# Neighbourhood attention: who scales and masks the bias tables, GpSimd or VectorE

## The chip, the cores and the metric

One core of a Trainium2 chip runs the whole program. The metric is the device time of one execution in microseconds; the lower the better. TensorE (PE) multiplies matrices out of SBUF into PSUM, VectorE (DVE), ScalarE (ACT) and GpSimd (POOL) work elementwise, and SyncE (SP) issues the transfers. Each engine runs its own instructions in the order in which they were written; between engines, semaphores are counted up and waited for.

## The reference, cut to what matters

The program computes two transformer blocks on 512 tokens. The change touches one stage of the second layer of the first block, in which eight heads of dense attention (C) and eight heads of neighbourhood attention (D) run. The D heads add a relative-position bias to their scores and mask columns out of the window:

```
col_valid = (c[None, :] >= c0[:, None]) & (c[None, :] < c0[:, None] + D_WIN_C)
valid = jnp.tile(col_valid, (1, wr))
...
s = jnp.einsum('bqhd,bkhd->bhqk', q_row, k_win,
               preferred_element_type=jnp.float32) * scale
row_idx = r0 + jnp.arange(wr) - r + (D_WIN_R - 1)
bias = rpb_f[:, row_idx[None, :, None], col_idx[:, None, :]]
s = jnp.where(valid, s + bias.reshape(H, GRID_W, wr * GRID_W)[None], NEG)
p = jax.nn.softmax(s, axis=-1).astype(v.dtype)
return jnp.einsum('bhqk,bkhd->bqhd', p, v_win)
```

The kernel adds a table to the raw scores, (bias / scale) + mask, with the mask 0 or -1e30, and multiplies by scale afterwards.

## The kernel before, in words

`attention` (L1679) runs 32 units. A unit is two heads (a group) and one quarter (128) of the 512 queries. Groups 0 to 3 are the C heads (units 0 to 15), groups 4 to 7 the D heads (units 16 to 31). A unit passes through the engines as follows; every engine's order is fixed by a loop over i.

- TensorE: `score(i)` (L1745) into PSUM, then `turn(i-2)` (L1757), the transposition of the probabilities of unit i-2, which waits until they are scaled, then `values` (L1772), a quarter of the product with V of an older group. `score(u)` needs the maxima of unit u-2 (D heads) or its exponentials (C heads).
- VectorE: `peak(i)`, the row maxima. For a C unit that is two reductions (L1867) and a small multiplication (L1871); for a D unit two fused instructions (L1861) that read the scores in PSUM and the bias table in SBUF and write the sum to SBUF, each followed by a short read of the accumulator. Then `scale_rows(i-1)`: a reciprocal (L1876) and two multiplications in place in SBUF, one for each head (L1879, 128 rows by 512 columns each); I call the two the scaling pair of unit i-1. Once in four units it also copies a finished group out (L1899).
- ScalarE: the copy of transposed probabilities (L1811), then the exponentials of unit i (L1826).

The bias tables are 8 heads of 128 x 896 float32 (448 KB each). They lie in four slots of the buffer `bias`. SyncE issues heads 0 to 3 at the stage's start, and heads 4 and 5, and 6 and 7, once the maxima of the group that used the slots before are done (L1905 to L1912). Heads 0 and 1 belong to group 4 (units 16 to 19), heads 2 and 3 to group 5, 4 and 5 to group 6 (from unit 24), 6 and 7 to group 7 (from unit 28).

Before the change, VectorE turns each table into (bias / scale) + mask itself, in `shape_bias` (L1837 to L1843), one instruction for each head. It stands behind `peak(i)` and ahead of `scale_rows(i-1)`, at i = 14 and 15 for heads 0 and 1, 18 and 19 for heads 2 and 3, 22 and 23, 26 and 27. GpSimd does nothing in this stage. In the whole program it has 22 small instructions: constants at the start, 16 copies of 128 x 2 in the first attention stage (L1729), and two memsets much later (L3685, L3686).

Of the kernel before, what the change touches and what calls it, by code (L numbers as in the profile page):

```python
# [17 lines left out]
ALU = mybir.AluOpType  # L18
# [4 lines left out]
P = 128  # L23
# [10 lines left out]
GRID = 64  # L34
WIN_C = 16
REL = 14
# [1256 lines left out]
class Net:  # L1293
# [385 lines left out]
    def attention(self, groups, kb, opened, evac, fill=None, weights=None, late=None):  # L1679
# [7 lines left out]
        s, ps = self.s, self.ps  # L1687
        g, sets = len(groups[0].q), 4 // len(groups[0].q)
        units = [(p, qt) for p in range(len(groups)) for qt in range(4)]
        n = len(units)  # L1690
        shaped = [groups[p].shaped for p, _ in units]
        nk = groups[0].k[0][0].shape[-1] // P
        bias_heads = [h for gr in groups for h in gr.bias or ()]
        with ExitStack() as ctx:
            tag, p = self.names, self.place
# [4 lines left out]
            bs = p(f'bias{tag}', [P, 4, REL * GRID], kb + 6.5 * g * nk) if bias_heads else None  # L1700
# [12 lines left out]
            def width(u):  # L1713
                k0, k1 = span(u)
                return (k1 - k0) * P

            @block.gpsimd
            def _(pool):
                done = 0
                for u, (p, qt) in enumerate(units):  # L1720
                    gr = groups[p]
                    if gr.sink is None:
                        continue
                    if not done:
                        pool.wait_ge(*s['copied'].at(sum(gr.sink is not None for gr in groups)))
                    if shaped[u - 2]:
                        pool.wait_ge(*s['exped'].at(u - 1))
                    w, at = width(u), 2 * sum(gr.sink is not None for gr in groups[:p])
                    pool.tensor_copy(sb[:, u % 2, :, w], ns[:, at:at + 2]).then_inc(*s['pool'].up())  # L1729
                    done += 1  # L1730
# [100 lines left out]
            @block.vector  # L1831
            def _(dve):
                sinks = [gr.sink for gr in groups if gr.sink is not None]
                for i, sink in enumerate(sinks):
                    dve.tensor_scalar(ns[:, 2 * i:2 * i + 2], sink, -1.0, None, ALU.mult).then_inc(*s['copied'].up())

                def shape_bias(p, j):  # L1837
                    h = groups[p].bias[j]
                    dve.wait_ge(*s[f'biasin{h % 4}'].at(16 * (h // 4 + 1)))
                    v = bs[:, h % 4, :].rearrange("p (a b) -> p a b", b=GRID)  # L1840
                    m = self.c('colmask')[:, None, :].to_broadcast([P, REL, GRID])
                    dve.scalar_tensor_tensor(out=v, in0=v, scalar=1.0 / groups[p].scale, in1=m, op0=ALU.mult,
                                             op1=ALU.add).then_inc(*s['vec'].up())  # L1843

                def peak(u):
                    p, qt = units[u]
                    gr, w = groups[p], width(u)
                    dve.wait_ge(*s['scored'].at(u + 1 - opened))
                    if shaped[u]:
                        if u >= 2 and shaped[u - 2]:  # L1850
                            dve.wait_ge(*s['exped'].at(u - 1))
                    for j in range(g):
                        src = ps[:, bank(u, j), 0:w]
                        if shaped[u]:
                            a = (6 - 2 * qt) * GRID
                            add = bs[:, gr.bias[j] % 4, a:a + w] if gr.bias else gr.mask(qt)
                            first = -NEG
                            if gr.sink is not None:
                                at = 2 * sum(gr.sink is not None for gr in groups[:p])
                                first = ns[:, at + j:at + j + 1]  # L1860
                            dve.tensor_tensor_reduce(sb[:, u % 2, j, 0:w], src, add, -gr.scale, first, ALU.add, ALU.min,  # L1861
                                                     stat_of(u, 1, j)).then_inc(*s['maxed' if j == g - 1 else 'vec'].up())
                        elif gr.folded:
                            dve.tensor_reduce(stat_of(u, 1, j), src, AX.X, ALU.max,
                                              negate=True).then_inc(*s['maxed' if j == g - 1 else 'vec'].up())
                        else:
                            dve.reduce_max(stat_of(u, 0, j), src, AX.X).then_inc(*s['vec'].up())  # L1867
                    if shaped[u] or gr.folded:
                        return
                    dve.wait_ge(*s['vec'].now())  # L1870
                    dve.tensor_scalar(stat(u, 1), stat(u, 0), -gr.scale, None, ALU.mult).then_inc(*s['maxed'].up())  # L1871

                def scale_rows(u):
                    gr, w = groups[units[u][0]], width(u)
                    dve.wait_ge(*s['exped'].at(u + 1))
                    dve.reciprocal(stat(u, 3), stat(u, 2)).then_inc(*s['vec'].up())  # L1876
                    dve.wait_ge(*s['vec'].now())
                    for j in range(g):
                        ins = dve.tensor_scalar(pr[:, u % 3, j, 0:w], pr[:, u % 3, j, 0:w], stat_of(u, 3, j), None, ALU.mult)  # L1879
                    ins.then_inc(*s['scaled'].up())  # L1880

                for i in range(n + 6):
                    if i < n:
                        peak(i)
                    if i + 2 < n and units[i + 2][1] in (0, 1) and groups[units[i + 2][0]].bias:
                        shape_bias(units[i + 2][0], units[i + 2][1])
                    if evac and i == 2:
                        evac.dve(dve, evac.late)
                    if late and i in (2, 3):
                        late[1](dve, i - 2)  # L1890
                    if 0 <= i - 1 < n:
                        scale_rows(i - 1)
                    p, part = divmod(i - 6, 4)
                    if weights and i == n:
                        weights(dve)
                    if p >= 0 and part == 3:
                        dve.wait_ge(*s['weighted'].at(p + 1))
                        for at, dst in groups[p].dst:
                            ins = dve.tensor_copy(dst, ps[:, at, :])  # L1899
                        ins.then_inc(*s['headout'].up())  # L1900
                self.last_head = len(groups[-1].dst), s['headout'].at(len(groups))
                self.mem_free = self.last_head[1]
# [2122 lines left out]
```

## Time and profile before

| | |
|---|---|
| time, median of 3 runs | 2836.95 us (2836.83 to 2837.25) |
| the profiled execution's own time | 2837.87 us |
| its span | 2836.6 us |
| granted TensorE clock, mean | 0.999 |
| TensorE busy | 2789.8 us (98% of the span) |
| VectorE busy | 1673.1 us (59%) |
| GpSimd busy | 5.0 us, 22 instructions |
| the attention stage of the change, from its first unit in `attention` to its last product | 879.3 to 991.8 us |

The profiled execution took 2837.87 us: its span of 2836.6 us and 1.27 us around it. It lies 0.92 us above the median of the runs. A row of a timeline gives start and duration in us, engine, line, operation, the buffers written and read, shapes, and in brackets how long the engine stood idle before it and what ended that. Where one row covers two instructions (x2), the duration is from the start of the first to the end of the second; on VectorE the second can start a little before the first is through.

### The profile page before, as it was taken

To read this page: it belongs to the slowest core of one execution; us is meant where nothing else is said; L and a number is where in the kernel's file an instruction comes from. 1 tells how busy PE (TensorE), PEld (TensorE's weight loads), DVE (VectorE), ACT (ScalarE), POOL (GpSimd) and SP (SyncE) were. 2 spreads that over 40 slices of the span, in tenths; PEclk is the share of its full clock that TensorE was granted. 3 is DMA by queue.
4 is the path that set the end of the run, shared out by engine and by line. 5 is a ranking of instruction groups with operands and counts; after the bars stand their busy time and mean duration, and the time that the engine had idled before them with its cause. 6 is when DMAs were issued, how large, how long until landed. Compare 5 with 4: busy or idle time off the path is not lost.

```text
span 2836.6 us, 38710 instructions
## 1 busy us (share of the span) xinstructions
PE 2789.8 (98%) x15838; PEld 2059.1 (73%) x15838; DVE 1673.1 (59%) x3425; ACT 651.4 (23%) x1349; POOL 5.0 (0%) x22
## 2 busy tenths in 40 slices
PE   9999999999999999999999999999999999999998
PEld 3557588888644486788887557777776877788887
DVE  5686554453344874655754876766656536766654
ACT  5651310100134613211100022522221102222200
POOL 0000000000000000000000000000000000000000
PEclk9999999999999999999999999999999999999999
DMA  4013122222221132222222122211113321222222
GB/s 150 30 39 118 52 82 90 89 97 90 91 73 55 34 119 75 75 89 89 90 89 97 61 68 75 97 52 48 48 46 134 118 91 53 81 90 89 85 93 82
DMA packets 63535, 228.59 MB, mean 81 GB/s; under 512 B 7168, under 2 KB 9472, under 8 KB 62592
## 3 DMA queue, kind: packets, MB, share of 16 engines
q1 hardware_dynamic: 63360, 226.14, 23.5%
q8 instruction: 125, 2.05, 0.3%
q14 instruction: 50, 0.41, 0.0%
HBM read 221.91 MB, written 4.19 MB: 80 GB/s over the span
## 4 chain that ended last, share of the span: by engine, by line
PE 93%; DVE 5%; issue 1%; ACT 0%; DMA 0%; SPq 0%; DVEq 0%; ACTq 0%
PE ps L1990 30%; PE ps L711 19%; PE ps L1385 9%; PE ps L2026 8%; PE ps L1397 5%; PE ps L1772 3%; PE ps L1745 2%; PE ps L1428 2%; PE ps L1466 2%; PE ps L1757 2%; PE ps L743 1%; PE ps L2574 1%; PE ps L2595 1%; PE ps L2805 1%; PE ps L3494 1%
## 5 line engine op out<-in xcount | busy, mean ns | idle before, releaser
L1990 PE MATMUL ps<-h,ring 128*128 128x256 f32 x1136 | 269.0, 380 | 3.9 <-ACT q_p L2124 2.0
L1990 PEld LDWEIGHTS ps<-h,ring 128*128 128x128 f32 x1136 | 214.9, 190 | 37.9 <-issue 8.7
L1990 PE MATMUL ps<-h_sums,w_sums 128*128 128x256 f32 x1008 | 224.4, 379 | 0.0
L1990 PEld LDWEIGHTS ps<-h_sums,w_sums 128*128 128x128 f32 x1008 | 191.5, 190 | 26.0
L711 PE MATMUL ps<-hid_sums,d_sums 128*128 128x256 f32 x740 | 175.8, 379 | 0.5 <-DVE hid_sums L1949 0.5
L711 PEld LDWEIGHTS ps<-hid_sums,d_sums 128*128 128x128 f32 x740 | 140.5, 190 | 19.9 <-issue 0.8
L1931 DVE TENSOR_TENSOR d_sums<-ring 128x512 f32<-128x512 f32 (+1 forms) x51 | 33.6, 659 | 167.8 <-DMA ring<-stream_dram 167.6
L1990 PE MATMUL ps<-c_h_sums,c_sums 128*128 128x256 f32 x504 | 112.2, 379 | 0.0
L967 ACT ACTIVATE d_xsq<-x 128x512 f32<-128x512 f32 x47 | 28.1, 621 | 363.2 <-DVE x L928 354.9
L1757 PEld LDWEIGHTS ps<-constants,probs 128*128 128x128 f32 x560 | 62.4, 141 | 62.2 <-DVE probs L1879 47.5
L1990 PEld LDWEIGHTS ps<-c_h_sums,c_sums 128*128 128x128 f32 x504 | 95.8, 190 | 13.0
L1385 PE MATMUL ps<-h,ring 128*128 128x512 f32 x240 | 104.9, 593 | 0.0
L1811 ACT ACTIVATE probsT<-ps 128x512 f32<-128x512 f32 (+2 forms) x176 | 82.8, 508 | 90.9 <-PE ps L1757 90.5
L1757 PE MATMUL ps<-constants,probs 128*128 128x128 f32 x560 | 82.7, 279 | 10.3 <-DVE probs L1879 9.6
L711 PE MATMUL ps<-hid_sums,ring 128*128 128x256 f32 x370 | 87.9, 379 | 0.0
L1385 PEld LDWEIGHTS ps<-h,ring 128*128 128x128 f32 x240 | 45.5, 190 | 56.9 <-issue 56.1
L711 PE MATMUL ps<-hid,ring 128*128 128x256 f32 x352 | 82.5, 379 | 0.0
L711 PE MATMUL ps<-hid,d_sums 128*128 128x256 f32 x352 | 82.5, 379 | 0.0
L3911 DVE SCALAR_TENSOR_TENSOR c_conv<-c_x,vectors,c_conv 128x511 f32<-128x511 f32 (+1 forms) x88 | 62.1, 747 | 34.1 <-ACT c_conv L3859 33.3
L1990 PE MATMUL ps<-h_sums,ring 128*128 128x256 f32 x336 | 79.4, 379 | 0.0
L1990 PE MATMUL ps<-h,w_sums 128*128 128x256 f32 x336 | 79.4, 379 | 0.0
L711 PEld LDWEIGHTS ps<-hid_sums,ring 128*128 128x128 f32 x370 | 70.3, 190 | 9.6
(724 smaller groups left out, 5215.1 us busy)
## 6 DMA issues: line engine op xcount, KB each, us to landing
ring<-stream_dram SPq DMA_DIRECT2D x395, 512.0 KB, 3.8
bias<-bias_dram SPq DMA_DIRECT2D x8, 448.0 KB, 4.5
mem<-mem_dram SPq DMA_DIRECT2D x3, 1024.0 KB, 5.7
x_kept_dram<-x SPq DMA_DIRECT2D x1, 2048.0 KB, 10.1
x<-x_kept_dram SPq DMA_DIRECT2D x1, 2048.0 KB, 7.8
out_dram<-x SPq DMA_DIRECT2D x16, 128.0 KB, 1.9
x<-x_dram SPq DMA_DIRECT2D x3, 512.0 KB, 7.8
rope_ab<-ropes_dram SPq DMA_DIRECT2D x4, 256.0 KB, 8.0
```

Source lines behind the costliest of these rows:

```text
L711: mm = pe.matmul(self.region(q, at), w(j), x(k), start=opens, stop=last and j == len(ks) - 1, skip_group_check=True)
L1385: mm = pe.matmul(out, w, r, start=(k == 0), stop=(k == len(rhs) - 1))
L1397: mm = pe.matmul(out, w, r, start=(k == 0), stop=(k == len(rhs) - 1))
L1428: mm = pe.matmul(out, l, w, start=(k == 0), stop=(k == len(lhs) - 1))
L1466: mm = pe.matmul(self.ps[:, m % 4, :], self.next_block(pe), src[k], start=(k == 0), stop=(k == len(src) - 1))
L1745: mm = pe.matmul(ps[:, bank(u, j), 0:(k1 - k0) * P], gr.q[j][i][:, qt * P:(qt + 1) * P], gr.k[j][i][:, k0 * P:k1 * P], start=(i == 0), sto ...
L1757: mm = pe.transpose(ps[:, turn_bank(u, j), b * P:(b + 1) * P], pr[:, u % 3, j, b * P:(b + 1) * P], self.c('ident'))
L1772: mm = pe.matmul(ps[at:at + rows, to, c], gr.v(b, j)[i], pt[:, p % 2, j, b, c], start=(b == 0), stop=(b == nk - 1), skip_group_check=True)
L1811: ins = act.activation(pt[:, p % 2, j, k0:k1, qt * P:(qt + 1) * P], ps[:, turn_bank(u, j), 0:(k1 - k0) * P].rearrange("p (b q) -> p b q", ...
L1990: mm = pe.matmul(ps[:, bank + at, 0:256], w(k), x(k), start=start and k == 0, stop=k == 3, skip_group_check=not start)
L2026: mm = pe.matmul(ps[:, bank, part], w(k), x(k), start=n in (0, 2) and k == 0, stop=k == 3, skip_group_check=True)
L3911: ins = dve.scalar_tensor_tensor(out=out, in0=xs[:, f % 2, j, 0:S - lag], scalar=self.v('conv', (2 - lag) * 2 * FT + FT * j + f), in1=out, ...
```

## The change

VectorE's `shape_bias` goes, and with it its eight instructions. GpSimd now walks through all eight heads in order, at the head of its part of the stage: it waits for the head's transfer, multiplies the table in place by 1/scale, waits for that, and adds the mask in place. VectorE waits for the second of a group's two heads at the group's first `peak`.

```
             @block.gpsimd
             def _(pool):
+                for gr in groups:
+                    for h in gr.bias or ():
+                        pool.wait_ge(*s[f'biasin{h % 4}'].at(16 * (h // 4 + 1)))
+                        v = bs[:, h % 4, :].rearrange("p (a b) -> p a b", b=GRID)
+                        pool.tensor_scalar(v, v, 1.0 / gr.scale, None, ALU.mult).then_inc(*s['pool'].up())
+                        pool.wait_ge(*s['pool'].now())
+                        pool.tensor_tensor(v, v, self.c('colmask')[:, None, :].to_broadcast([P, REL, GRID]),
+                                           ALU.add).then_inc(*s['biased'].up())
...
-                def shape_bias(p, j):
-                    h = groups[p].bias[j]
-                    dve.wait_ge(*s[f'biasin{h % 4}'].at(16 * (h // 4 + 1)))
-                    v = bs[:, h % 4, :].rearrange("p (a b) -> p a b", b=GRID)
-                    m = self.c('colmask')[:, None, :].to_broadcast([P, REL, GRID])
-                    dve.scalar_tensor_tensor(out=v, in0=v, scalar=1.0 / groups[p].scale, in1=m, op0=ALU.mult,
-                                             op1=ALU.add).then_inc(*s['vec'].up())
-
                 def peak(u):
                     p, qt = units[u]
                     gr, w = groups[p], width(u)
                     dve.wait_ge(*s['scored'].at(u + 1 - opened))
+                    if gr.bias and qt == 0:
+                        dve.wait_ge(*s['biased'].at(bias_heads.index(gr.bias[1]) + 1))
...
                 for i in range(n + 6):
                     if i < n:
                         peak(i)
-                    if i + 2 < n and units[i + 2][1] in (0, 1) and groups[units[i + 2][0]].bias:
-                        shape_bias(units[i + 2][0], units[i + 2][1])
```

On VectorE, where the C units end and the D units begin (i = 14 to 16), this stood before; `stats` holds the maxima and sums, `probs` the probabilities, `shaped` the sums of scores and bias, and an ISA row with `ps,bias` is one of the fused instructions of `peak`:

```order
L1871 TENSOR_SCALAR stats_5551<-stats_5551 128x2 [waits vec]
L1842 SCALAR_TENSOR_TENSOR bias_5550<-bias_5550,constants 128x896 [waits biasin0]
L1876 RECIPROCAL stats_5551<-stats_5551 128x2 [waits exped]
L1879 TENSOR_SCALAR probs_5547<-probs_5547,stats_5551 128x512 [waits vec]
L1879 TENSOR_SCALAR probs_5547<-probs_5547,stats_5551 128x512
L1867 TENSOR_REDUCE stats_5551<-ps 128x1 [waits scored]
L1867 TENSOR_REDUCE stats_5551<-ps 128x1
L1871 TENSOR_SCALAR stats_5551<-stats_5551 128x2 [waits vec]
L1842 SCALAR_TENSOR_TENSOR bias_5550<-bias_5550,constants 128x896 [waits biasin1]
L1876 RECIPROCAL stats_5551<-stats_5551 128x2 [waits exped]
```

The same place now (the lines have moved down by two):

```order
L1873 TENSOR_SCALAR stats_5551<-stats_5551 128x2 [waits vec]
L1878 RECIPROCAL stats_5551<-stats_5551 128x2 [waits exped]
L1881 TENSOR_SCALAR probs_5547<-probs_5547,stats_5551 128x512 [waits vec]
L1881 TENSOR_SCALAR probs_5547<-probs_5547,stats_5551 128x512
L1869 TENSOR_REDUCE stats_5551<-ps 128x1 [waits scored]
L1869 TENSOR_REDUCE stats_5551<-ps 128x1
L1873 TENSOR_SCALAR stats_5551<-stats_5551 128x2 [waits vec]
L1878 RECIPROCAL stats_5551<-stats_5551 128x2 [waits exped]
L1881 TENSOR_SCALAR probs_5547<-probs_5547,stats_5551 128x512 [waits vec]
L1881 TENSOR_SCALAR probs_5547<-probs_5547,stats_5551 128x512
L1863 ISA shaped_5549,stats_5551<-ps,bias_5550 128x512 [waits biased,scored]
```

The reciprocal and the scaling pair now follow directly on the maxima, and the first fused instruction of the group has taken on the wait for `biased`.

On GpSimd nothing stood between the copies of the first attention stage and the memsets. Now there stands (heads 0 and 1 shown; heads 2 to 7 follow in the same form, ahead of the memsets):

```order
L1737 COPY shaped_607<-sinks_609 128x2 [waits exped] x14
L1723 ISA
L1723 TENSOR_SCALAR bias_5550<-bias_5550 128x896 [waits biasin0]
L1725 TENSOR_TENSOR bias_5550<-bias_5550,constants 128x896 [waits pool]
L1723 TENSOR_SCALAR bias_5550<-bias_5550 128x896 [waits biasin1]
L1725 TENSOR_TENSOR bias_5550<-bias_5550,constants 128x896 [waits pool]
```

Eight instructions of VectorE have become sixteen of GpSimd, and one without a buffer (the ISA row) stands ahead of them with nothing to wait for. The orders of TensorE, ScalarE and SyncE are as before.

## Rows read from the trace of the kernel before

**Rows 1.** The page: busy time of an engine, and the chain that ended last.
```profile
PE 2789.8 (98%) x15838; PEld 2059.1 (73%) x15838; DVE 1673.1 (59%) x3425; ACT 651.4 (23%) x1349; POOL 5.0 (0%) x22
...
PE 93%; DVE 5%; issue 1%; ACT 0%; DMA 0%; SPq 0%; DVEq 0%; ACTq 0%
```

**Rows 2.** Timeline of TensorE, the scores of units 16 to 21.
```profile
928.69 1.13 PE L1745 MATMUL ps<-k_d,q_d 64*128 64x512 f32 x4
...
932.48 1.13 PE L1745 MATMUL ps<-k_d,q_d 64*128 64x512 f32 x4
...
935.57 1.13 PE L1745 MATMUL ps<-k_d,q_d 64*128 64x512 f32 x4
...
938.66 1.13 PE L1745 MATMUL ps<-k_d,q_d 64*128 64x512 f32 x4
...
942.14 1.13 PE L1745 MATMUL ps<-k_d,q_d 64*128 64x512 f32 x4
...
945.36 1.13 PE L1745 MATMUL ps<-k_d,q_d 64*128 64x512 f32 x4
```

**Rows 3.** Timeline of VectorE at i = 15: a table, then the scaling pair.
```profile
928.32 1.08 DVE L1842 SCALAR_TENSOR_TENSOR bias<-bias,constants 128x896 f32<-128x896 f32 x1
...
929.51 0.88 DVE L1879 TENSOR_SCALAR probs<-probs,stats 128x512 f32<-128x512 f32 x2
```

**Rows 4.** Groups of instructions, 870 to 990 us: busy us, mean ns.
```profile
L1879 DVE TENSOR_SCALAR probs<-probs,stats 128x512 f32<-128x512 f32 x62 | 27.3, 483 | 1.1
...
L1842 DVE SCALAR_TENSOR_TENSOR bias<-bias,constants 128x896 f32<-128x896 f32 x8 | 8.7, 1087 | 0.0
...
L1899 DVE COPY q_c<-ps 128x512 f32<-128x512 f32 x4 | 2.7, 682 | 0.0
```

**Rows 5.** Timeline of GpSimd: its longest instruction.
```profile
1691.53 1.81 POOL L3686 MEMSET gla_att<- 128x2048 f32 x1
```

**Rows 6.** Timeline of VectorE beside that instruction.
```profile
1691.96 0.27 DVE L3607 MEMSET gla_state<- 128x256 f32 x1
1692.14 0.63 DVE L2049 TENSOR_TENSOR rw_sums<-ring 128x512 f32<-128x512 f32 x1
```

**Rows 7.** Busy time by stretch (PE, PEld, DVE, ACT, POOL), clock, DMA share, GB/s.
```profile
884.00:886.00 2.00, 1.67 (x10) 1.32 (x11) 1.93 (x6) 1.04 (x4) 0.00 (x0) 1.00 0.29 117
...
945.00:947.00 2.00, 2.00 (x11) 0.89 (x10) 1.09 (x3) 1.94 (x6) 0.00 (x0) 1.00 0.11 40
```

**Rows 8.** The tile `bias`: transfers from issue to landing, all eight.
```profile
DMA to landing us min/median/max: 3.4/4.5/6.7
```

**Rows 9.** Timeline of VectorE: the scaling pairs of units 1 to 4.
```profile
883.39 0.88 DVE L1879 TENSOR_SCALAR probs<-probs,stats 128x512 f32<-128x512 f32 x2
...
885.77 0.88 DVE L1879 TENSOR_SCALAR probs<-probs,stats 128x512 f32<-128x512 f32 x2
...
888.77 0.88 DVE L1879 TENSOR_SCALAR probs<-probs,stats 128x512 f32<-128x512 f32 x2
...
891.55 0.88 DVE L1879 TENSOR_SCALAR probs<-probs,stats 128x512 f32<-128x512 f32 x2
```

**Rows 10.** Timeline of TensorE: the turns of units 1 to 4, and of unit 20.
```profile
884.33 1.09 PE L1757 MATMUL ps<-constants,probs 128*128 128x128 f32 x8 [0.57 <-DVE probs L1879]
...
886.98 1.04 PE L1757 MATMUL ps<-constants,probs 128*128 128x128 f32 x8
...
889.75 1.04 PE L1757 MATMUL ps<-constants,probs 128*128 128x128 f32 x8
...
892.49 1.09 PE L1757 MATMUL ps<-constants,probs 128*128 128x128 f32 x8
...
949.51 1.09 PE L1757 MATMUL ps<-constants,probs 128*128 128x128 f32 x8
```

**Rows 11.** Timeline of VectorE: the scaling pair of unit 20, and unit 24's first fused instruction.
```profile
947.96 0.88 DVE L1879 TENSOR_SCALAR probs<-probs,stats 128x512 f32<-128x512 f32 x2
...
956.20 0.69 DVE L1861 CUSTOM_DVE_ANT_0 shaped<-ps,bias 128x512 f32<-128x512 f32 x1
```

## The prediction

> **What bounds the kernel now.** I read the page first. TensorE is busy for 98% of the span, the chain that ended last runs through it for 93% and through VectorE for 5%, and transfers have no share [rows 1]. So a microsecond is won or lost only where TensorE waits, and what is won in one stage stays won, as no transfer stands behind it in the chain.
>
> Then the timeline of TensorE in the changed stage, taken by the starts of its scores. In the D heads a unit takes 3.09 us where nothing disturbs it (935.57 to 938.66). It takes more at the places of `shape_bias`: units 16 to 17 take 3.79, units 19 to 20 3.48 and 20 to 21 3.22 [rows 2]. These are excesses of 0.70, 0.39 and 0.13 us. The last two come again in the same size at heads 4 and 5 and at 6 and 7, a pattern that I read three times. The timeline of VectorE shows why: 1.08 us of table stand directly ahead of the scaling pair at 929.51, whose end at 930.39 TensorE's turn waits for [rows 3].
>
> Last I read the stage's start (879 to 893 us), where TensorE has no products with V yet and its units are short. There turns 1 to 4 begin 0.06, 0.33, 0.10 and 0.06 us behind the end of the scaling pair that they need (pairs start at 883.39, 885.77, 888.77, 891.55 and last 0.88; turns start at 884.33, 886.98, 889.75, 892.49) [rows 9, 10]. Nothing can be slipped into VectorE there. This matters since the first four tables land just then.
>
> **What is removed.** Eight instructions of 1.09 us, 8.7 us of VectorE [rows 4]. On TensorE's path lie 0.70 + 3 x (0.39 + 0.13) = 2.26 us [rows 2]. Without the table at i = 15, the pair starts some 1.0 us sooner, at 928.5, ends at 929.4, and turn 14 can follow its score 16 (928.69 and 1.06 of it) at 929.75. What is late next is nothing: TensorE's own 3.09 us a unit bound it, as between units 18 and 19. The remaining 6.4 us of the 8.7 stood in VectorE's idle time and are worth nothing.
>
> **What is added on GpSimd.** Sixteen instructions of 128 x 896. No row shows one that reads a tensor of this size. The nearest row of the engine is a memset of 128 x 2048 in 1.81 us, 0.88 ns a column [rows 5]: 0.79 us for one pass over 896 columns. The nearest row of the shape is VectorE's own 1.09 us [rows 4]. Lower bound for each kind: 0.79. Upper bound, if each operand and the result were a pass by itself: two passes, 1.6 us, for the multiplication, and three, 2.4 us, for the addition. I take 0.9 for the multiplication (between the two nearest rows) and twice that, 1.8, for the addition, which reads two operands; with 0.1 for the wait between them, 2.8 us a head, against bounds of 1.7 and 4.1.
>
> The Trainium skill ("GPSIMD Engine Reference", section "Elementwise — side-by-side cycle accounting") gives an addition of two tensors some 2.6 cycles a column at 1.2 GHz; an estimate by it is 1.94 us for 896 columns. With it every meeting with an addition, below, would be up to 0.14 us dearer. No run here shows it.
>
> The instruction without a buffer ahead of them on GpSimd has 700 us of idle time before the first table, and costs nothing, whatever it does. The memsets behind them wait for 1691 us anyway [rows 5].
>
> **When they run.** The four first tables are 1.8 MB, and the transfers are through at 884.6 us (29% of the stretch from 884) [rows 7]. The first can land 3.4 us after its issue at 877.3 [rows 8]; I take 881 us. From there GpSimd is busy to some 895, exactly beside the stage's start. Heads 4 and 5 land by 945.2 (11% of the stretch from 945) [rows 7] and are wanted at 956.20 [rows 11]: 11 us for 5.6 us of work, hidden. Heads 6 and 7 have the same room, 13 us later. Units 16 and 24 wait for `biased`, which has come long before; behind this wait would stand the pair of the unit before, and TensorE behind that.
>
> **The disputed cost: both engines in SBUF at once.** The scaling pair goes from SBUF to SBUF: two instructions of 0.48 us in 0.88 us, so one in 0.40 [rows 3, 4]. A copy of the same 512 columns out of PSUM takes 0.68 alone [rows 4]. So the pair moves data at nearly twice the rate, by a second way into SBUF that the other forms do not use. Whether that way is free while GpSimd reads, no row shows. The nearest rows are VectorE's fast memset (0.18 us from start to start for 256 columns) and an addition of 0.63 us, both undisturbed beside GpSimd's memset [rows 6]; but that one only writes. Bounds: nothing, or every pair waits until the running GpSimd instruction is through, and between its halves for another one. I take the middle: a pair that meets a running instruction waits for its end, then passes whole. The reason is the pair's rate, which the undisturbed addition does not have; the memset's evidence lowers the chance, not the size.
>
> The Trainium skill ("SBUF — State Buffer", section "Who interferes with whom") says that VectorE in a two-port mode and GpSimd take turns on a shared pair of ports, each for a whole instruction, and that copies and multiplications by a scalar from SBUF to SBUF enter such a mode. By it the sum is the one below; without it, 2834.7. The undisturbed rows 6 do not contradict it where it speaks of two SBUF inputs (these collide only with reads of GpSimd), and no row tests the rest.
>
> Walked through at the start, with 0.9 and 1.8:
> - GpSimd: multiplication 881.0 to 881.9, addition to 883.8. Pair 1, due 883.39, waits 0.41; turn 1 is 0.35 late.
> - GpSimd, after that pair: 884.7 to 885.6, 885.7 to 887.5. Pair 2, due 885.77 + 0.41 = 886.2, waits 1.3, is 1.7 late; turn 2 had 0.33 of room: 1.4 late.
> - GpSimd: 888.4 to 889.3, 889.4 to 891.2. Pair 3, due 888.77 + 1.4 = 890.2, waits 1.0; turn 3 is 2.3 late.
> - GpSimd: 892.1 to 893.0, 893.1 to 894.9. Pair 4, due 891.55 + 2.3 = 893.9, waits 1.0; turn 4 is 3.3 late. The first four tables are done.
>
> So +3.3 us, never given back, as TensorE bounds what follows. In the D heads the pair of unit 20 ends at 948.84 and its turn starts at 949.51, a room of 0.67 [rows 10, 11]. Two pairs in each of two stretches meet GpSimd. A pair falling at random into an addition of 1.8 us costs beyond its room 1.13 x 1.13 / 2 / 1.8 = 0.35 us on average, and additions are two thirds of GpSimd's time: 0.25 a pair, 1.0 for four (0 to 4.5).
>
> **The sum.** -2.3 + 3.3 + 1.0 = +2.0 us. On the profiled execution that is 2837.87 + 2.0 = 2839.9 us; the median of the runs stands 0.92 lower, so 2839.0 us.
>
> **Rivals.**
> - No contest in SBUF. Then the gain stands alone: 2836.95 - 2.3 = 2834.7 us. For it: rows 6. Against it: the pair's doubled rate. If GpSimd alone gave way, the result is the same, since it has 11 us for 5.6.
> - GpSimd gets in between the halves of a pair. This ends on the other side. A GpSimd instruction that has waited during the first half starts before the second. From pair 1 on each pair then passes two instructions of GpSimd: the rest of one (about 1.0) and a whole one (0.9 or 1.8, mean 1.35), 3 x 2.35 = 7.0 for pairs 2 to 4, and 0.4 + 0.9 for pair 1, less 0.5 of room: 7.8 us. In the D heads two stretches cost 1.5 each. Sum: -2.3 + 7.8 + 3.0 = +8.5, so 2845.4 us. It counts as slower once the waits pass 8.0 us. For it: GpSimd's request is the older one. Against it: the second half starts 0.08 us before the first is through, so VectorE may never let go.
> - Tables late. Four instructions must fit between 945.2 and 956.20; more than 5.4 us a head, above my upper bound of 4.1 unless GpSimd itself is held up, would stop unit 24. At 6.0 it costs 1.2 in each of two stretches: 2836.95 - 2.3 + 2.4 = 2837.1 without any other wait, and about 2846 with the waits of the rival before.
>
> **How the numbers follow.** Forecast 0.43, with a range of its own from 2837 to 2842.5. No contest 0.33. Between the halves 0.20. Late tables 0.03. Something else 0.01. The range 2834.4 to 2846.0 holds the first three but for the upper half of the third, where GpSimd's durations lie near their upper bounds (1.6 and 2.4 instead of 0.9 and 1.8 would make each wait a third longer or more). About what a measurement of this kernel can tell from no change is 0.2%, 5.7 us. Faster by more than that needs a gain over 5.7 us, and only 2.26 are there: 0.02. Slower by more: most of the third case, and the upper end of the fourth and first: 0.21. Within: 0.77.
>
> **What would show it.** In the profile after: (1) the D units at 3.09 us from score to score at the places where 3.79, 3.48 and 3.22 stood; wrong if VectorE is late there for another reason. (2) GpSimd at 0.8 to 1.6 and 0.8 to 2.4 us an instruction. (3) For the forecast: the pairs of units 1 to 4 start late, or their instructions last over 0.48 us, each ending behind a GpSimd instruction, and TensorE idles some 3 us more between 884 and 896. If all 62 keep 0.48 us while GpSimd runs, the first rival holds. If the two halves of a pair lie more than 0.5 us apart with a GpSimd instruction between them, the second. (4) Units 24 and 28 show no wait for GpSimd; one would be the last rival. The prediction as a whole is wrong if a stage outside 879 to 992 us changes its length.

## The result and the profile after

The changed kernel takes 2850.02 us (median of 6 runs, 2848.23 to 2851.29) against 2837.06 us (6 runs, 2836.74 to 2837.25) for the one before: a ratio of 1.0046, 95% interval 1.0035 to 1.0056. It is 13.0 us slower where +2.0 was forecast with a range up to 2846.0. The profiled execution took 2850.39 us, its span 2848.9 us, 12.3 more than before. The first line of its page and the groups of the stage, over 870 to 1000 us (busy us, mean ns), answer to [rows 1, 4]:

```profile
PE 2791.8 (98%) x15838; PEld 2059.9 (72%) x15838; DVE 1684.2 (59%) x3417; ACT 651.3 (23%) x1349; POOL 41.9 (1%) x38
```
```profile
L1881 DVE TENSOR_SCALAR probs<-probs,stats 128x512 f32<-128x512 f32 x62 | 45.6, 777 | 1.1
...
L1723 POOL TENSOR_SCALAR bias<-bias 128x896 f32<-128x896 f32 x8 | 20.1, 2511 | 763.4 <-DMA bias<-bias_dram 763.0
...
L1725 POOL TENSOR_TENSOR bias<-bias,constants 128x896 f32<-128x896 f32 x8 | 16.8, 2102 | 0.7
```

VectorE lost eight instructions and is busy for 11 us more; the mean of the multiplications of the scaling pairs has gone from 483 to 777 ns. On GpSimd the multiplication takes 2.5 us and the addition 2.1.

The timelines of GpSimd and of VectorE at the stage's start:

```profile
880.69 2.45 POOL L1723 TENSOR_SCALAR bias<-bias 128x896 f32<-128x896 f32 x1 [704.05 <-DMA bias<-bias_dram]
883.22 2.12 POOL L1725 TENSOR_TENSOR bias<-bias,constants 128x896 f32<-128x896 f32 x1
885.42 2.51 POOL L1723 TENSOR_SCALAR bias<-bias 128x896 f32<-128x896 f32 x1
888.01 2.12 POOL L1725 TENSOR_TENSOR bias<-bias,constants 128x896 f32<-128x896 f32 x1
```
```profile
882.34 1.08 DVE L1881 TENSOR_SCALAR probs<-probs,stats 128x512 f32<-128x512 f32 x1
...
883.34 2.28 DVE L1881 TENSOR_SCALAR probs<-probs,stats 128x512 f32<-128x512 f32 x1
...
887.12 3.29 DVE L1881 TENSOR_SCALAR probs<-probs,stats 128x512 f32<-128x512 f32 x2
```

The two halves of the first pair are shown singly. The first is taken up at 882.34 and is through at 883.42, 0.28 us behind the end of GpSimd's multiplication (883.14). The second is taken up at 883.34, but GpSimd's addition has stood ready since 883.22. The addition goes first, ends at 885.34, and the half is through at 885.62, again 0.28 us behind it. The next pair has the same picture 4.8 us later. A pair lasts 3.3 us instead of 0.88 [rows 9], and a unit takes 4.8 us, the time of one head on GpSimd. TensorE, turns of units 1 to 4, then a product with V:

```profile
885.68 1.09 PE L1765 MATMUL ps<-constants,probs 128*128 128x128 f32 x8 [3.10 <-DVE probs L1881]
...
890.47 1.09 PE L1765 MATMUL ps<-constants,probs 128*128 128x128 f32 x8 [0.43 <-DVE probs L1881]
...
895.27 1.09 PE L1765 MATMUL ps<-constants,probs 128*128 128x128 f32 x8 [1.99 <-DVE probs L1881]
...
900.07 1.66 PE L1765 MATMUL ps<-constants,probs 128*128 128x128 f32 x8 [1.99 <-DVE probs L1881]
901.66 1.98 PE L1780 MATMUL ps<-probsT,v_c 128*64 128x512 f32 x4
```

The last two rows are slow by themselves (1.66 where 1.09 is usual, 1.98 where 1.08). The stretches show why; their last columns are the granted clock, the share of the transfers and GB/s:

```profile
888.00:890.00 2.00, 2.00 (x3) 0.34 (x1) 2.00 (x2) 1.23 (x4) 1.99 (x1) 0.50 0.00 0
...
902.00:904.00 2.00, 2.00 (x5) 0.42 (x2) 0.40 (x2) 2.00 (x6) 0.00 (x0) 0.54 0.01 4
```

A granted clock of 0.50 is TensorE at 1.2 GHz instead of 2.4. It fell behind the idle time of 3.10 us and once more behind the two of 1.99. The first fall lies in a wait for VectorE and costs nothing (the idle time at 890.47 is only 0.43 for that reason); the second lengthens the stage.

In the D heads, the scores of units 16, 17 and 20 to 24, which answer to [rows 2], and among them the two turns that waited:

```profile
937.86 1.13 PE L1753 MATMUL ps<-k_d,q_d 64*128 64x512 f32 x4
...
940.95 1.13 PE L1753 MATMUL ps<-k_d,q_d 64*128 64x512 f32 x4
...
950.22 1.13 PE L1753 MATMUL ps<-k_d,q_d 64*128 64x512 f32 x4
...
953.32 1.13 PE L1753 MATMUL ps<-k_d,q_d 64*128 64x512 f32 x4
...
956.46 1.13 PE L1753 MATMUL ps<-k_d,q_d 64*128 64x512 f32 x4
...
959.20 1.09 PE L1765 MATMUL ps<-constants,probs 128*128 128x128 f32 x8 [1.60 <-DVE probs L1881]
...
961.23 1.13 PE L1753 MATMUL ps<-k_d,q_d 64*128 64x512 f32 x4
...
963.28 1.09 PE L1765 MATMUL ps<-constants,probs 128*128 128x128 f32 x8 [0.93 <-DVE probs L1881]
...
965.32 1.13 PE L1753 MATMUL ps<-k_d,q_d 64*128 64x512 f32 x4
```

The gain is there: 3.09 us from unit 16 to 17 where 3.79 stood, and 3.10 from 20 to 21 where 3.22 stood. But units 22 to 23 take 4.77 and 23 to 24 take 4.09, beside heads 4 and 5 on GpSimd; the same comes again beside heads 6 and 7.

Here a pair also meets the beginning of a multiplication on GpSimd (VectorE, GpSimd):

```profile
952.83 1.55 DVE L1881 TENSOR_SCALAR probs<-probs,stats 128x512 f32<-128x512 f32 x2
```
```profile
953.05 2.57 POOL L1723 TENSOR_SCALAR bias<-bias 128x896 f32<-128x896 f32 x1 [53.32 <-DMA bias<-bias_dram]
```

The pair is through at 954.38, while the multiplication runs until 955.62. So a half does not always wait for GpSimd's instruction to end. The section on the hardware comes back to this.

For the comparisons I cut the stage in two in the timeline of TensorE. The start runs from the score of unit 2 (879.28 before, 878.11 after) to that of unit 16 (928.69, 937.86). The rest runs on to the last row of products with V, sixteen at once (988.17, 1000.55). Behind the stage nothing changed: from that row to the span's end it is 1848.4 us in both. Start and rest are read from one profiled execution of each kernel, so they and the medians need not add up to the last microsecond. For e7_only_add the profiled execution, 2841.40 us, is the fastest of ten; for e5_one_after it is 1.0 us above the median.

| kernel | time, us | against the kernel before, us | start, us | rest, us |
|---|---|---|---|---|
| before | 2837.06 | | 49.41 | 59.48 |
| changed | 2850.02 | +13.0 | 59.75 | 62.69 |
| e1_no_shaping | 2835.27 | -1.5 | 49.41 | 57.23 |
| e2_both | 2855.43 | +18.7 | 58.87 | 67.99 |
| e4_accum_before | 2843.97 | +7.2 | 51.16 | 64.17 |
| e4_accum_after | 2842.29 | +5.5 | 55.68 | 58.58 |
| e8_all_slow | 2836.98 | +0.2 | 50.65 | 58.59 |
| e5_one_before | 2840.38 | +3.5 | 50.41 | 62.07 |
| e5_one_after | 2842.78 | +5.9 | 57.02 | 59.27 |
| e6_later | 2844.42 | +7.5 | 53.94 | 62.70 |
| e3_memsets | 2843.32 | +6.6 | 54.00 | 61.52 |
| e7_only_add | 2843.17 | +6.4 | 54.15 | 59.69 |
| v2_early | 2834.50 | -2.4 | 49.41 | 57.23 |
| v2_again | 2834.58 | -2.2 | 49.41 | 57.24 |

Times are medians; the kernel before ran anew beside each group of experiments (2836.75, 2836.89 and 2836.76 us).

### The profile page after: what moved, and what is told of

It is laid out like the page before. It is cut to its first block, busy times and chain, and to the rows that moved or that the text cites. A ratio compares the mean times of both kernels' runs of the same rounds, so it can differ in the third digit from the quotient of the medians.

```text
span 2848.9 us, 38721 instructions
## 1 busy us (share of the span) xinstructions
PE 2791.8 (98%) x15838; PEld 2059.9 (72%) x15838; DVE 1684.2 (59%) x3417; ACT 651.3 (23%) x1349; POOL 41.9 (1%) x38
## 4 chain that ended last, share of the span: by engine, by line
PE 93%; DVE 5%; issue 1%; ACT 0%; DMA 0%; SPq 0%; DVEq 0%; ACTq 0%
PE ps L1990 30%; PE ps L711 19%; PE ps L1385 9%; PE ps L2026 8%; PE ps L1397 5%; PE ps L1780 3%; PE ps L1753 2%; PE ps L1428 2%; PE ps L1466 2%; PE ps L1765 2%; PE ps L743 1%; DVE probs L1881 1%; PE ps L2574 1%; PE ps L2595 1%; PE ps L2805 1%
## 5 line engine op out<-in xcount | busy, mean ns | idle before, releaser
L1881 DVE TENSOR_SCALAR probs<-probs,stats 128x512 f32<-128x512 f32 (+2 forms) x176 | 88.5, 533 | 4.0
```

## The experiments

The theory after the result: VectorE's fast form of multiplication (0.40 us for 512 columns from SBUF to SBUF) and GpSimd take turns in SBUF, and all of the loss comes from these waits. The main rivals: the wait for `biased` (late tables), the moved order on VectorE, and a fixed price of TensorE's lower clock.

**e1_no_shaping: no engine makes the tables.** Against the kernel before:

```
+                    if gr.bias and qt == 0:
+                        for h in gr.bias:
+                            dve.wait_ge(*s[f'biasin{h % 4}'].at(16 * (h // 4 + 1)))
...
-                    if i + 2 < n and units[i + 2][1] in (0, 1) and groups[units[i + 2][0]].bias:
-                        shape_bias(units[i + 2][0], units[i + 2][1])
```

> No engine scales and masks the tables: the eight instructions of VectorE are gone and nothing is put on GpSimd; VectorE only waits for the transfers (the scaling by 1/scale and the column mask are left out of the computation). Theory (turns in SBUF: VectorE's removal is worth 2.26 us, and the loss comes from GpSimd's instructions): 2.3 us faster than before, 2834.8 us, D units at 3.09 us throughout. Rival (what VectorE's order or the added waits do is the loss): slower than before, by up to 13 us.

Measured 2835.27 us, ratio 0.9995 (0.9985 to 1.0004). The interval cannot tell it from before, and the median lies 1.5 us under where 2.3 were expected. The trace is clearer: the rest of the stage is 2.25 us shorter (57.23 against 59.48), the start the same. So in the stage the removal is worth what the forecast said, and the order on VectorE is not the loss.

**e2_both: the tables stay on VectorE, and GpSimd does the same work for nobody.**

```
+                for gr in groups:
+                    for h in gr.bias or ():
+                        pool.wait_ge(*s[f'biasin{h % 4}'].at(16 * (h // 4 + 1)))
...
+                        pool.tensor_scalar(spare[:, :], self.cst[:, 0:REL * GRID], 8.0, None, ALU.mult).then_inc(*s['pool'].up())
+                        pool.wait_ge(*s['pool'].now())
+                        v = spare[:, :].rearrange("p (a b) -> p a b", b=GRID)
+                        pool.tensor_tensor(v, v, self.c('colmask')[:, None, :].to_broadcast([P, REL, GRID]),
+                                           ALU.add).then_inc(*s['biased'].up())
```

> The kernel before, with VectorE's shaping in place, and beside it GpSimd does sixteen instructions of the same two forms and size at the same times, from the constants into a spare buffer that nobody reads or waits for. Theory (turns in SBUF): GpSimd alone costs what the changed kernel lost plus the gain: 13 + 2.3 = some 15 us slower than before (2852 us), with scaling pairs of 3.3 us at units 1 to 4. Rival (tables late, or the wait for 'biased'): nobody waits for GpSimd here, so the time is that of before, 2837 us.

Measured 2855.43 us, +18.7 (ratio 1.0065, 1.0050 to 1.0080), against some 15 expected. Nobody waits for GpSimd here by a semaphore, and all of the loss is there. The surplus over 15 lies in the rest of the stage. VectorE's own table instructions, with two inputs in SBUF each, wait as well: two of the eight met an addition of GpSimd and took 2.62 and 2.63 us. Groups of that kernel; the means were 483 and 1087 ns before [rows 4]:

```profile
L1890 DVE TENSOR_SCALAR probs<-probs,stats 128x512 f32<-128x512 f32 x62 | 42.9, 734 | 1.1
...
L1853 DVE SCALAR_TENSOR_TENSOR bias<-bias,constants 128x896 f32<-128x896 f32 x8 | 11.8, 1470 | 0.0
```

**e4_accum_before and e4_accum_after: the pair in a slower form.** The same edit on the kernel before and on the changed one:

```
-                        ins = dve.tensor_scalar(pr[:, u % 3, j, 0:w], pr[:, u % 3, j, 0:w], stat_of(u, 3, j), None, ALU.mult)
+                        acc = dict(scalar2=0.0, op1=ALU.add, accum_out=stat_of(u, 4, j)) if bias_heads else dict(scalar2=None)
+                        ins = dve.tensor_scalar(pr[:, u % 3, j, 0:w], pr[:, u % 3, j, 0:w], stat_of(u, 3, j), op0=ALU.mult, **acc)
```

> The kernel before with the same other form of the scaling pair: the control. Both theories: each pair 0.4 to 0.5 us longer, which only costs where TensorE waits for it (the first four units, and the units beside a table): 2 to 5 us over before, 2839 to 2842 us.

> The changed kernel with the scaling pair of this stage in another form: each multiplication also adds a zero and sums its row into an unused statistic. Theory (only the fast form, 0.40 us for 512 columns, has to take turns with GpSimd): the pair runs at 0.6 us each, does not wait for GpSimd, and the time is within 1 us of e4_accum_before minus 2.3 us. Rival (every instruction of VectorE that reads and writes SBUF waits for GpSimd): 10 us or more above e4_accum_before.

The control costs 7.2 us (expected 2 to 5): a half takes 0.74 us, and VectorE is short of time beside each table. With the pairs in this form the changed kernel is 1.7 us faster than its control, 2842.29 against 2843.97. All 62 halves keep 744 ns in both, GpSimd or not. What still waited at the start was an instruction I had not thought of, the multiplication of the maxima, 128 x 2 (timelines of VectorE and GpSimd in e4_accum_after):

```profile
888.01 1.93 DVE L1873 TENSOR_SCALAR stats<-stats 128x2 f32<-128x2 f32 x1
```
```profile
887.84 2.07 POOL L1725 TENSOR_TENSOR bias<-bias,constants 128x896 f32<-128x896 f32 x1
```

It takes 0.17 us alone and is through 0.03 us behind GpSimd's addition. TensorE keeps its full clock in this run (1.00 in every stretch of 2 us from 880 to 920), and the start still costs 4.5 us more than its control's, 55.68 against 51.16: the waits cost time without any fall of the clock.

**e8_all_slow: that one in the slower form too** (the pairs as in e4_accum_after).

```
-                    dve.tensor_scalar(stat(u, 1), stat(u, 0), -gr.scale, None, ALU.mult).then_inc(*s['maxed'].up())
+                    acc = dict(scalar2=0.0, op1=ALU.add, accum_out=stat_of(u, 4, 0)) if bias_heads else dict(scalar2=None)
+                    dve.tensor_scalar(stat(u, 1), stat(u, 0), -gr.scale, op0=ALU.mult, **acc).then_inc(*s['maxed'].up())
```

> e4_accum_after, with the small multiplication of the C units' maxima (128 x 2) in the slower form too. In e4_accum_after that multiplication was the only instruction of VectorE that still waited (up to 1.9 us) and the start still cost some 3.5 us more than in its control. Theory (only the fast form takes turns, whatever its size): no instruction of VectorE waits for GpSimd any more, and the time falls from 2842.3 to 2838 to 2839 us, 5 us under e4_accum_before, which pays for its tables on VectorE. Rival (something else at the start waits for GpSimd): it stays at 2842 us.

Measured 2836.98 us, 7.0 under its control, e4_accum_before (5 were expected), and level with the kernel before (ratio 1.0001, 0.9991 to 1.0010). GpSimd does all its sixteen instructions in this run. The start falls from 55.68 to 50.65 us. Groups:

```profile
L1883 DVE TENSOR_SCALAR_CACHE_REDUCE probs<-probs,stats 128x512 f32<-128x512 f32 x62 | 43.8, 744 | 1.1
...
L1723 POOL TENSOR_SCALAR bias<-bias 128x896 f32<-128x896 f32 x8 | 19.6, 2451 | 752.9 <-DMA bias<-bias_dram 752.5
...
L1874 DVE TENSOR_SCALAR_CACHE_REDUCE stats<-stats 128x2 f32<-128x2 f32 x14 | 2.2, 155 | 0.5
```

This settles the cause: with the same work on GpSimd at the same time, no wait for it is left once VectorE's fast form is gone. The halves keep the 744 ns of the control, and the start is no longer than there (50.65 against 51.16). A kernel in this form with no tables at all was not run.

**e5_one_before and e5_one_after: the pair as one instruction.**

```
+                    if bias_heads:
+                        ins = dve.tensor_tensor(pr[:, u % 3, :, 0:w], pr[:, u % 3, :, 0:w],
+                                                stat(u, 3)[:, :, None].to_broadcast([P, g, w]), ALU.mult)
-                    for j in range(g):
+                    for j in () if bias_heads else range(g):
```

> The kernel before with the scaling pair as that one instruction: the control. Both theories: 0.25 us longer a unit on VectorE, 0 to 2 us over before.

> The changed kernel with the scaling pair of this stage as one instruction that multiplies both heads by their reciprocals (two inputs in SBUF, 1024 columns, about 1.1 us). Theory (a turn is taken for each instruction, and GpSimd gets in between the halves): one instruction waits once, for the rest of one GpSimd instruction (up to 2.5 us) and no more; the loss against e5_one_before is about half of the changed kernel's, 3 to 7 us. Rival (two inputs in SBUF need no turn): 2 us faster than e5_one_before. Rival (the wait is for all of GpSimd's work in hand): as slow as the changed kernel, 2850 us.

The control costs 3.5 us (expected 0 to 2); the changed kernel in this form is 2.4 above its control (expected 3 to 7). Its start loses 6.6 us (57.02 against 50.41) where the pairs in halves lost 10.3. How much of that is one wait instead of two, this run cannot say, since the edit changes the form as well. The pair at 885.42 is through at 887.39, 0.44 us ahead of the end of GpSimd's multiplication (885.38 to 887.83), so it did not wait for that end; and up to 1.4 us at a time went to the multiplication of the maxima, which is still in the fast form. 1.65 us of the 6.6 are the lower clock (0.50 in 898 to 900). In the D heads GpSimd's multiplication was stretched, so far that unit 24 waited for its tables, the last rival of the forecast (e5_one_after, VectorE, then GpSimd):

```profile
885.42 1.97 DVE L1881 TENSOR_TENSOR probs<-probs,stats 128x1024 f32<-128x1024 f32 x1
...
962.26 0.69 DVE L1863 CUSTOM_DVE_ANT_0 shaped<-ps,bias 128x512 f32<-128x512 f32 x1 [2.07 <-POOL bias L1725]
```
```profile
950.02 3.20 POOL L1723 TENSOR_SCALAR bias<-bias 128x896 f32<-128x896 f32 x1 [50.64 <-DMA bias<-bias_dram]
```

**e6_later: heads 0 to 3 in the quiet part of the C units.**

```
+                        if h == 0:
+                            pool.wait_ge(*s['exped'].at(2))
+                            for _ in range(2):
...
+                            pool.wait_ge(*s['exped'].at(9))
```

(The lines left out are a multiplication and an addition on a spare buffer.)

> The changed kernel, but GpSimd starts with heads 0 to 3 only after the exponentials of unit 8, when the C units run at 3.80 us and a scaling pair ends 1.13 us before its turn. Ahead of that, while VectorE is idle (869 to 880 us), GpSimd runs two multiplications and two additions of the same size on a spare buffer. Theory (turns): pairs are still stretched to 3.3 us, 2.4 more, of which 1.1 is room: 1.3 us for each of four or five units, so the start costs 5 to 7 us instead of 10.3, and the whole is 2844 to 2847 us. Rival (the start is dear because TensorE falls to its lower clock there): the same 10 us are lost wherever the tables are made. The four instructions alone show what GpSimd takes without VectorE: theory of turns, some 2.4 and 1.8 us, since the 2.1 of the additions then holds a wait for half a pair; rival, 2.5 and 2.1 as beside VectorE.

Measured 2844.42 us, within the expected 2844 to 2847; the start loses 4.5 us (expected 5 to 7) instead of 10.3, and the rest is as in the changed kernel, 62.70 against 62.69. So the price depends on the place. But the time came out in part by luck, as the waits were not those expected: only the first pair was stretched to 3.4 us, the next two lasted 1.56 (at 911.91 and 916.60), and the multiplication of the maxima waited instead (1.80 us at 919.39). The clock fell here too (0.50 in 910 to 912); the product and the score that it stretched, by 0.45 and 1.20 us, are 1.65 of the 4.5. GpSimd's instructions alone:

```profile
867.45 2.45 POOL L1725 TENSOR_SCALAR spare<-constants 128x896 f32<-128x896 f32 x1 [691.00 <-ACT probs L1845]
869.98 2.07 POOL L1728 TENSOR_TENSOR spare<-spare,constants 128x896 f32<-128x896 f32 x1
```

They take 2.45 and 2.07 us with VectorE idle (it has nothing between 866.9 and 879.8). My 1.8 for the addition was wrong: 2.07 is its own time, and GpSimd is hardly held up by the pairs.

**e3_memsets: GpSimd only writes.** The kernel before, with four fills for each head:

```
+                        pool.wait_ge(*s[f'biasin{h % 4}'].at(16 * (h // 4 + 1)))
+                        pool.memset(spare[:, :], 0.0).then_inc(*s['pool'].up())
+                        pool.wait_ge(*s['pool'].now())
...
```

> The kernel before, and beside it GpSimd fills a spare buffer, four fills of 128 x 896 for each head in place of the multiplication and the addition: it writes and reads nothing (0.8 us each, 3.2 us a head against 4.7). Theory (the fast form needs both ways in and out of SBUF, so any work of GpSimd takes turns with it): the scaling pairs of units 1 to 4 wait up to 0.8 us for each half, 0.5 to 1 us each unit, and the time is 2 to 6 us over before. Rival (only reads of GpSimd are in the way, as the fast fill of VectorE ran undisturbed beside GpSimd's memset): pairs keep 0.88 us and the time is that of before.

Measured 2843.32 us, +6.6 (ratio 1.0023, 1.0014 to 1.0032), a little over the expected 2 to 6; a pair of its start (VectorE) beside a fill of GpSimd:

```profile
889.61 2.16 DVE L1891 TENSOR_SCALAR probs<-probs,stats 128x512 f32<-128x512 f32 x2
```
```profile
889.59 0.84 POOL L1725 MEMSET spare<- 128x896 f32 x1
```

The fast form waits for writes as well. The table instruction of VectorE does not: its eight keep a mean of 1086 ns, and one that began with a fill (955.07, the fill from 955.08 to 955.92) took 1.08 us, where in e2_both two that met an addition took 2.6. The clock stayed at 1.00 in the whole stage, and the start lost 4.6 us all the same. That VectorE's own fast fill ran undisturbed beside GpSimd's memset [rows 6] said nothing about the pairs.

**e7_only_add: the addition alone.** The multiplication on GpSimd and the wait behind it are left out:

```
-                        pool.tensor_scalar(v, v, 1.0 / gr.scale, None, ALU.mult).then_inc(*s['pool'].up())
-                        pool.wait_ge(*s['pool'].now())
```

> The changed kernel with the addition of the mask alone on GpSimd; the multiplication by 1/scale is left out of the computation. GpSimd's work falls from 4.7 to 2.2 us a head. Theory (turns): the loss goes with the number and length of GpSimd's instructions: about 4 us at the start instead of 10.3, 1 instead of 2.7 in each of the two later stretches, less the gain of 2.3: 3 to 5 us over before, 2840 to 2842 us. Rival (a fixed price for having GpSimd in the stage): near 2850 us.

Measured 2843.17 us, +6.4 where 3 to 5 were expected. The start loses 4.7 us and the rest 2.5 against e1_no_shaping: about half of the changed kernel's 10.3 and 5.5, as GpSimd's time has halved. So the loss follows the time that GpSimd works and is not a fixed price for having it in the stage. One part does not follow it: TensorE's clock fell once (0.50 in 886 to 888) and stretched a turn and a score by 0.78 and 0.95 us, together 1.7, near the 1.6 of the changed kernel.

**v2_early: the tables on VectorE at better places.** The kernel before, with `shape_bias` behind the scaling pair instead of ahead of it, heads 0 to 3 at i = 10 to 13, heads 4 to 7 at 22, 23, 26 and 27 (left out: the wait for the tables at a group's first `peak`, and the old call of `shape_bias`):

```
+                early = [(p, j, 10 + 2 * (p - first) + j if p < first + 2 else 4 * p - 2 + j)
+                         for p in range(first, len(groups)) for j in range(g)]
...
                     if 0 <= i - 1 < n:
                         scale_rows(i - 1)
+                    for p, j, at in early:
+                        if i == at:
+                            shape_bias(p, j)
```

> VectorE makes the tables, as before, but at other places: behind the scaling pair instead of ahead of it, heads 0 to 3 at i = 10 to 13, where VectorE has 1.32 us of idle time in each C unit, and heads 4 and 5 at i = 22 and 23, 6 and 7 at i = 26 and 27. Theory (the 2.26 us were lost only because a table stood ahead of a pair that was wanted): 1.5 to 2.3 us faster than before, 2834.7 to 2835.5 us. Rival (VectorE is short of time in the stage): as before.

> v2_early once more, in more rounds, for the size of its gain: VectorE makes the tables behind the scaling pair, heads 0 to 3 early. Theory: 2.3 us under before, as in the first run (2834.5 against 2836.9). Rival (the first run's difference was noise): within 1 us of before.

Measured 2834.50 us, ratio 0.9992 (0.9983 to 1.0002), and again 2834.58 us, 0.9992 (0.9983 to 1.0001): 2.4 and 2.2 us under the kernel before. Each interval just reaches no change, but the two runs agree with each other and with the trace. There the stage is as short as with no tables at all, 49.41 and 57.23 us (scores of units 16 and 17):

```profile
927.18 1.13 PE L1745 MATMUL ps<-k_d,q_d 64*128 64x512 f32 x4
930.27 1.13 PE L1745 MATMUL ps<-k_d,q_d 64*128 64x512 f32 x4
```

It is the fastest kernel here that computes the whole reference, and it leaves GpSimd idle.

## Why the prediction was wrong

**What bounds the kernel, and the gain: right.** 2.26 us were forecast; e1_no_shaping and v2_early show 2.25 in the rest of the stage, and 1.5 and 2.4 in the medians. In the changed kernel, units 16 to 17 run at 3.09 us.

**The disputed cost: the right mechanism, and the wrong step in it.** Contest in SBUF was forecast, and it decides: e2_both has it without any dependence, e8_all_slow has the dependence without the contest. The step that failed is "a pair that meets a running instruction waits for its end, then passes whole". Each half waits by itself, and GpSimd gets in between, as the rival on the other side had it (chance 0.20, 2845.4 us). My reason against that rival, that the second half is taken up before the first is through, holds in the rows (883.34 against 883.42) and did not help: GpSimd's addition had been ready 0.12 us longer (883.22) and went first. In the D heads the step fails the other way too: there halves got through before GpSimd's multiplication had ended (954.38 against 955.62). The Trainium skill ("SBUF — State Buffer", section "Who interferes with whom") has the exclusive turn for a whole instruction and the multiplication by a scalar among the forms that take it, and that the form which also writes its accumulator does not. The runs agree with the last two (3.3 us instead of 0.88 a pair; 744 ns kept). With the whole instruction they agree for GpSimd's additions and fills (a half is through 0.28 us behind their end), but not for its multiplication, within which halves got through; there the measurement decides. The rule counts instructions. Read strictly, two halves are two turns, and that I had not followed through.

**GpSimd's durations: wrong for the multiplication.** I took 0.9 us, with an upper bound of 1.6 from two passes at the memset's rate [rows 5]; it takes 2.45, more than the addition with two inputs (2.07, within its bounds of 0.8 to 2.4). A head takes 4.7 us instead of 2.8 (bounds 1.7 to 4.1). A memset's rate was no bound for it.

**The start: 3.3 us forecast, 10.3 measured.** By the rows: turn 1 comes 7.57 us after the score of unit 2 instead of 5.05, so 2.5. Turns 1 to 4 then take 3 x 4.80 us instead of 8.16 in all, so 6.2. TensorE's lower clock stretches the turn, the product and the score behind it by 0.57, 0.90 and 0.13, so 1.6; the forecast had no term for the clock. Together 10.3. That the clock's part is paid is read from the rows of one execution; no run took it away alone. It is a consequence of the waits and not a rival to them: in e4_accum_after and e3_memsets, at full clock, the start lost 4.5 and 4.6 us. So the second wait within the pair, the durations and the clock all had a share; how the first two divide was not measured apart.

**The D heads: 1.0 us forecast, 5.5 measured** (62.69 against 57.23). Over the two stretches this is 2.7 each. Three pairs in each met GpSimd: one was stretched from 0.88 to 1.55 us, just the room of 0.67, and cost nothing; the next two, to 3.2 and to 2.2 us, cost 1.7 and 1.0. So the room was right. The average of 0.25 us a pair was mis-sized: it took one wait, for an addition of 1.8 us, and no second one.

**The sum.** -2.3 + 10.3 + 5.5 = +13.5 in the stage, against +13.0 in the medians. The range missed it as it bounded GpSimd's multiplication by the wrong row, and the rival's price with it, and as nothing in it stood for the clock. One sum of the forecast is wrong in itself: late tables with the waits of the rival before come to 2836.95 - 2.3 + 7.8 + 3.0 + 2.4 = 2847.9 us by its own terms, not about 2846. That case did not occur.

**Tables late: not in the changed kernel.** `biased` was waited for in e5_one_after only, 2.07 us, where GpSimd's work itself was held up, the condition named for it.

## What to carry to other kernels

Before elementwise work goes to GpSimd, look at what VectorE does at the same time: each fast instruction from SBUF to SBUF, however small, can wait for GpSimd's current instruction, for an addition or a fill until it is through, and two in a row can each wait anew. The price is what these waits take beyond the room at that place, and it is paid by whoever waits for VectorE. If VectorE has idle time in the stage, first try the work at another place of its own order: behind the instruction that is wanted and not ahead of it got the whole gain here.

## What the runs showed of the hardware that was not expected

- GpSimd multiplies a table of 128 x 896 float32 by a constant in 2.45 us and adds a second one in 2.07 to 2.12. VectorE does both in one instruction of 1.09.
- VectorE's multiplication of 128 x 2, 0.17 us alone, waited up to 1.9 us for GpSimd.
- GpSimd's multiplication does not hold the way from end to end. Small multiplications of VectorE (128 x 2) taken up within its first 0.7 us were through 0.95 us into it, 1.5 us ahead of its end (in e4_accum_after taken up at 880.88, beside one that began at 880.61, through at 881.56). Halves of a pair taken up at its beginning were through 1.2 to 1.4 us into it (the pair at 952.83 of the changed kernel). A half taken up 1.13 us into it took its usual 0.47 us (912.99 in e6_later, beside 911.86). Halves taken up 1.6 to 1.7 us into it waited for its end (882.34 in the changed kernel). Beside additions no half got through: each taken up during one was through 0.28 or 0.29 us behind its end. Only a small multiplication taken up 0.01 us behind the start of an addition (881.05 in e7_only_add) took its usual 0.17 us. No run tells why.
- VectorE's table instruction (two inputs in SBUF) waited for an addition of GpSimd (2.6 instead of 1.09 us in e2_both) and not for a fill (1.08 in e3_memsets).
- A multiplication of VectorE with two inputs (128 x 1024) and one of GpSimd hold each other up: VectorE's took 1.97 instead of 1.22 us, GpSimd's 3.20 instead of 2.45 (e5_one_after).
- TensorE fell to its lower clock (0.50 in 888 to 890) behind 3.1 us of idle time in the changed kernel, and did not in e4_accum_after, which idled up to 1.9 us at a time in the same stretch. In e5_one_after, which also idled no longer than 1.9 us at a time there, it fell to 0.50 (898 to 900). So the length of a single idle time does not tell these runs apart.
